# Half of a depthwise convolution moved from VectorE to GpSimd

## The chip, the cores and the metric

The kernel runs on one core of one Trainium2 chip. The metric is the device time of one execution in microseconds. Five engines work side by side on the core, each with its own instruction stream, and wait for each other through counted semaphores: TensorE (matmuls, PE in the profile; its weight loads are PEld), VectorE (DVE), ScalarE (ACT), GpSimd (POOL) and SyncE (SP), which here only issues the transfers of weights.

## The reference

The program is two transformer blocks in a row on 256 tokens of width 1024, all in float32. The second block has two layers and mixes tokens in four ways: Fourier, convolution, grouped attention, differential attention. The change touches only the convolution:

```python
def conformer_conv(z, w, bias, ln_g, ln_b):
    a, g = jnp.split(z, 2, axis=-1)
    u = a * jax.nn.sigmoid(g)                      # 256 tokens x 512 channels
    y = lax.conv_general_dilated(u, w[:, None, :], window_strides=(1,),
                                 padding=[(15, 15)],      # 31 taps
                                 feature_group_count=512) + bias
    return jax.nn.silu(layer_norm_2(y, ln_g, ln_b))

def mixer_stream(parts, ...):
    y_four = fourier_mix(zf) @ w_four              # branch 0
    y_conv = conformer_conv(...) @ w_conv          # branch 1
    ...                                            # branches 2 and 3: the attentions
    return sum(gates * [y_four, y_conv, y_gqa, y_diff]) @ w_out
```

Each channel has its own 31 weights (depthwise), and the layer norm runs over the 512 channels of a token.

## The kernel before

Activations lie transposed: channels on the 128 partitions, tokens along the free side, so 512 channels are four chunks of 128x256. Weights come in units of 128x2048 floats (1 MB), about 5.76 us of TensorE work each. Every product is made of three passes of a reduced float32 form: a value is split in a high part and a rest. For each weight unit ScalarE writes `w_high` (L343), VectorE writes `w_rest = raw - w_high` (L349), and TensorE multiplies high by high, high by rest and rest by high (L733). `w_high` has four buffers, `w_rest` two, so VectorE is at most one unit ahead.

The second block runs in passes: c0 (context, layer 0), x0 (tokens, layer 0), c1 (only keys and values) and x1 (tokens, layer 1). In c0, x0 and x1 ("full" passes) the order of the units is written by hand: conv_u, conv_g, four, q, kv, dq, dk, dv, gate0 (4 units), proj0 (2), gate1 (4), proj1 (2), then the attention "gqa", gate2, proj2, the attention "diff", gate3, proj3, out and the feed forward. `gateN` gives the gates of branch N, `projN` the projection of its result. Each engine has its own copy of this order, as calls of `linear(name, beside={unit: work})` (`cols_linear(..., before=...)` on TensorE): what stands in `beside` runs after the unit of that number.

The convolution: VectorE multiplies u by sigmoid (L2160), starts `acc` with the first tap and the bias for four chunks (L2163), and then does the other 30 taps as `acc += conv_in[shifted] * tap` with one scalar_tensor_tensor for each chunk and tap (L2087, in hardware loops, each waiting for the tap before it through `conv_step`). They are laid beside the units from four to proj0. When all are done (`taps_done`), TensorE sums `acc` over channels with a matrix of ones (L1167, `sum_acc`, ahead of gate1's unit 1), VectorE subtracts the mean (`conv_centre`, L2127 and L2128), ScalarE squares, TensorE sums again (`sum_squares`, ahead of unit 2), VectorE and ScalarE make the inverse root, VectorE scales (`conv_scale`), ScalarE applies silu, and `conv_split` (L2048) makes the operand of proj1. `merge_rows` multiplies the projection in the four PSUM banks with the gate (L1700) at the end of each branch; this frees the banks for the next unit.

In x0 and x1 gate1 also has the rotary embedding beside it (`swap_qk`, `rotate_q`, `rotate_d`). GpSimd builds tables in the first 225 us and later only writes rest parts of attention operands (L711). `rstd` is a 128x256 tile that norms use.

Of the kernel before, what the change touches and what calls it, by code (L numbers as in the profile page):

```python
# [136 lines left out]
def build(nc, t, out, consts):  # L137
    ctx = ExitStack()
    with ctx:
# [3 lines left out]
        def sem(name):  # L143
            return ctx.enter_context(nc.semaphore(name))
# [99 lines left out]
        def s5a(i):  # L244
# [62 lines left out]
        conv_a, conv_sig, conv_step, conv_st, conv_stc, conv_root, conv_n = [  # L307
            sem(x) for x in ("conv_a", "conv_sig", "conv_step", "conv_st", "conv_stc", "conv_root", "conv_n")]
# [187 lines left out]
        DVE_CHUNKS = HC  # L496
# [133 lines left out]
        def _(pool):  # L630
# [73 lines left out]

            for key in TASKS:
                for at in range(-1, len(TASKS[key])):
# [8 lines left out]
        def _(pe):  # L715
# [352 lines left out]
            for num, (p, l, s) in enumerate(PASSES):  # L1068
# [67 lines left out]
                def swap_dk():  # L1136
                    evacuated(pe, p + "dk")
                    pe.wait_ge(kd_dupc, num + 1)
                    pe.wait_ge(conv_n, 3 * nf + 2)
                    swap_halves(t1, HC, 2)  # L1140
# [29 lines left out]
                def sum_acc():  # L1170
                    pe.wait_ge(v_ready, num + 1)
                    conv_sums(1, acc, 0)

                def sum_squares():
                    conv_sums(2, oT, T)
# [6 lines left out]
                branch(0)  # L1182
                if rx is not None:
                    branch(1, gate_before={0: swap_qk, 1: sum_acc, 2: sum_squares, 3: lambda: (double_k(num), swap_dq())},
                           proj_before={1: swap_dk})
                    pe.wait_ge(d_rot, 3 * rx + 3)
                else:
                    branch(1, gate_before={1: sum_acc, 2: sum_squares, 3: lambda: double_k(num)})
# [28 lines left out]
        def _(act):  # L1217
# [262 lines left out]
            for num, (p, l, s) in enumerate(PASSES):  # L1480
# [73 lines left out]
                def conv_squares():  # L1554
                    act.wait_ge(conv_n, 3 * nf + 1)
                    A(oT, acc, ACT.Square).then_inc(conv_st, 1)
# [13 lines left out]
                branch(0)  # L1570
                branch(1, gate_beside={0: conv_squares, 1: conv_sqrt, 2: conv_silu, 3: lambda: doubled_out(num)})
# [33 lines left out]
        def _(dve):  # L1605
# [437 lines left out]
            for num, (p, l, s) in enumerate(PASSES):  # L2043
# [50 lines left out]
                def taps_done():  # L2094
# [70 lines left out]
                linear(p + "four", beside={0: lambda: taps(1, 2), 1: lambda: taps(3, 2)})  # L2165
                linear(p + "q", beside={0: lambda: taps(5, 2), 1: lambda: taps(7, 2)})
                linear(p + "kv", beside={0: lambda: taps(9, 2)})
                linear(p + "dq", beside={0: lambda: taps(11, 2), 1: lambda: (v_out(), taps(13, 2))})
                linear(p + "dk", beside={0: lambda: (fourier_split(), taps(15, 1)), 1: lambda: (mean_squares(), taps(16, 1))})
# [113 lines left out]
```

## Time and profile before

| | |
|---|---|
| median of 3 runs | 2777.2 us (2774.94 to 2777.76) |
| profiled execution | 2774.94 us, its span 2773.1 us |
| TensorE busy | 2354.6 us (85%) |
| VectorE busy | 1702.4 us (61%) |
| ScalarE busy | 1051.3 us (38%) |
| GpSimd busy | 278.4 us (10%) |
| taps on VectorE (L2087) | 360 instructions, 146.8 us busy, mean 477 ns |
| w_rest on VectorE (L349) | 311 instructions, 713.7 us busy, mean 2295 ns |
| chain that ended last | PE 67%, DVE 19%, ACT 4%, POOL 1% |

Busy is the time in which an engine executes; neighbouring instructions on one engine overlap a little in the records, so eight taps of 477 ns mean take 3.25 us. A wait is idle time of an engine, put down to the instruction that released it. The granted clock of TensorE is given as a share of 2.4 GHz: 1.0 or 0.5.

### The profile page before, as it was taken

To read this page: it belongs to the slowest core of one execution; us is meant where nothing else is said; L and a number is where in the kernel's file an instruction comes from. 1 tells how busy PE (TensorE), PEld (TensorE's weight loads), DVE (VectorE), ACT (ScalarE), POOL (GpSimd) and SP (SyncE) were. 2 spreads that over 40 slices of the span, in tenths; PEclk is the share of its full clock that TensorE was granted. 3 is DMA by queue.
4 is the path that set the end of the run, shared out by engine and by line. 5 is a ranking of instruction groups with operands and counts; after the bars stand their busy time and mean duration, and the time that the engine had idled before them with its cause. 6 is when DMAs were issued, how large, how long until landed. Compare 5 with 4: busy or idle time off the path is not lost.

```text
span 2773.1 us, 42565 instructions
## 1 busy us (share of the span) xinstructions
PE 2354.6 (85%) x17409; PEld 2181.0 (79%) x17409; DVE 1702.4 (61%) x2085; ACT 1051.3 (38%) x1202; POOL 278.4 (10%) x277
## 2 busy tenths in 40 slices
PE   4766688879999987769999988679999998776998
PEld 4621378879999987669999977479998997656998
DVE  5699734545548765555557965656545787555554
ACT  4200233444334444334344344334334435434432
POOL 3857200020000000100000001200000001110000
PEclk9878779979999998789999998779999999978999
DMA  5267624425555442135555432134545443113552
GB/s 164 94 268 307 240 94 139 150 65 169 182 191 157 143 148 69 56 120 168 181 175 153 152 106 67 40 98 153 182 161 158 152 146 98 61 45 108 171 178 91
DMA packets 282994, 388.31 MB, mean 140 GB/s; under 512 B 7847, under 2 KB 255966, under 8 KB 276703
## 3 DMA queue, kind: packets, MB, share of 16 engines
q1 hardware_dynamic: 279148, 379.40, 41.8%
q10 hardware_dynamic: 3282, 5.74, 0.6%
q8 instruction: 108, 1.77, 0.3%
q0 software_dynamic: 416, 1.08, 0.3%
q14 instruction: 40, 0.32, 0.0%
HBM read 385.04 MB, written 1.05 MB: 139 GB/s over the span
## 4 chain that ended last, share of the span: by engine, by line
PE 67%; DVE 19%; issue 4%; ACT 4%; POOL 1%; DVEq 0%; ACTq 0%
PE L L733 55%; PE M L733 5%; DVE w_rest L349 3%; DVE work L2087 2%; PE M L850 1%; POOL work_r L711 1%; DVE m L1891 1%; DVE gate L1891 1%; DVE work L2064 1%; DVE m L1706 1%; DVE gate L1700 1%; PE M L1092 1%; ACT w_high L343 1%; DVE work L2205 1%; PE L L877 1%
## 5 line engine op out<-in xcount | busy, mean ns | idle before, releaser
L733 PE MATMUL L<-n_high,w_high 128*128 128x256 f32 x3584 | 1055.0, 294 | 93.2 <-DVE n_rest L1644 42.2
L733 PE MATMUL L<-n_rest,w_high 128*128 128x256 f32 x3584 | 1039.9, 290 | 0.0
L733 PE MATMUL L<-n_high,w_rest 128*128 128x256 f32 x3584 | 1039.2, 290 | 0.0
L349 DVE TENSOR_TENSOR w_rest<-raw,w_high 128x2048 fp32r<-128x2048 f32 x311 | 713.7, 2295 | 382.9 <-PE L L733 347.9
L733 PEld LDWEIGHTS L<-n_high,w_high 128*128 128x128 f32 x3584 | 714.6, 199 | 115.6 <-issue 104.9
L343 ACT ACTIVATE w_high<-raw 128x2048 fp32r<-128x2048 f32 x311 | 594.0, 1911 | 502.7 <-PE L L733 432.2
L733 PEld LDWEIGHTS L<-n_rest,w_high 128*128 128x128 f32 x3584 | 715.3, 200 | 0.8
L733 PEld LDWEIGHTS L<-n_high,w_rest 128*128 128x128 f32 x3584 | 714.0, 199 | 0.0
L711 POOL TENSOR_TENSOR work_r<-kv,work_r 128x512 fp32r<-128x512 f32 (+2 forms) x44 | 63.6, 1449 | 2050.5 <-ACT work_r L1291 2050.5
L733 PE MATMUL M<-work_r 128*128 128x256 f32 (+3 forms) x744 | 170.8, 384 | 70.7 <-POOL work_r L711 35.6
L733 PEld LDWEIGHTS M<-work_r 64*128 64x128 f32 (+2 forms) x744 | 121.6, 215 | 106.8 <-issue 50.5
L733 PE MATMUL L<-hid_high,w_high 128*128 (+1 forms) x704 | 198.1, 281 | 6.1 <-DVE hid_rest L1988 6.1
L733 PE MATMUL L<-hid_rest,w_high 128*128 (+1 forms) x704 | 196.9, 280 | 0.0
L733 PE MATMUL L<-hid_high,w_rest 128*128 (+1 forms) x704 | 196.9, 280 | 0.0
L733 PE MATMUL L<-b_high,w_high 128*128 128x256 f32 x432 | 127.8, 296 | 50.0 <-ACT gate L1240 40.0
L2087 DVE SCALAR_TENSOR_TENSOR work<-work,tapc 128x256 f32<-128x256 f32 x360 | 146.8, 477 | 2.8 <-DVE work L2066 0.7
L733 PEld LDWEIGHTS L<-hid_high,w_high 128*128 128x128 f32 x704 | 134.3, 191 | 7.0 <-DVE hid_rest L1988 7.0
L1297 ACT ACTIVATE work<-M,soft 128x512 f32<-128x512 f32 (+1 forms) x104 | 62.6, 602 | 190.6 <-DVE soft L1716 190.5
L733 PEld LDWEIGHTS L<-hid_rest,w_high 128*128 128x128 f32 x704 | 134.0, 190 | 0.1
L733 PEld LDWEIGHTS L<-hid_high,w_rest 128*128 128x128 f32 x704 | 133.8, 190 | 0.0
L1716 DVE TENSOR_REDUCE soft<-M 128x1 f32<-128x512 f32 (+1 forms) x104 | 60.5, 586 | 118.7 <-PE M L733 118.7
L733 PEld LDWEIGHTS L<-b_high,w_high 128*128 128x128 f32 x432 | 87.3, 202 | 52.6 <-issue 41.7
(339 smaller groups left out, 2850.4 us busy)
## 6 DMA issues: line engine op xcount, KB each, us to landing
raw<-in_w_in SPq DMA_DIRECT2D x116, 1024.0 KB, 5.4
raw<-in_w_ffn SPq DMA_DIRECT2D x99, 1024.0 KB, 5.2
raw<-in_w_ada SPq DMA_DIRECT2D x48, 1024.0 KB, 8.1
raw<-in_w_out SPq DMA_DIRECT2D x16, 1024.0 KB, 5.0
raw<-in_w_gate SPq DMA_DIRECT2D x11, 1024.0 KB, 5.3
raw<-in_w_up SPq DMA_DIRECT2D x11, 1024.0 KB, 5.3
raw<-in_w_down SPq DMA_DIRECT2D x11, 1024.0 KB, 5.0
raw<-in_w_four SPq DMA_DIRECT2D x6, 1024.0 KB, 5.0
```

Source lines behind the costliest of these rows:

```text
L343: nc.scalar.activation(w_high[:, u.first % 4, :], raw[:, u.first % 4, :], ACT.Copy).then_inc(high_ready, 1)
L349: nc.vector.tensor_tensor(w_rest[:, u.first % 2, :], raw[:, u.first % 4, :], w_high[:, u.first % 4, :].bitcast(F32), ALU.subtract).then_in ...
L711: nc.gpsimd.tensor_tensor(rest, src, high.bitcast(F32), ALU.subtract).then_inc(op_rest, 1)
L733: ins = mm(dst, a, b, start=first and i == 0, stop=last and i == 2, skip_group_check=skip)
L850: ins = mm(M[:, 0, 0:T], ones[:, :], m[:, c, :], start=c == 0, stop=c == DC - 1)
L877: ins = nc.tensor.transpose(turned_bank[x["group"] % 2][:, c * P:(c + 1) * P], exps[(i - x["map"]) % 3][:, c * P:(c + 1) * P], ident[:, :])
L1092: ins = mm(M[:, c // 2, c % 2 * T:(c % 2 + 1) * T], y1[:, c, a, k * P:(k + 1) * P], dft256[:, k, a, :], start=i == 0, stop=i == 3)
L1297: A(exps[i % 3][:, 0:nk], score_bank[x["g"] % 2][:, 0:nk], ACT.Exp, bias=soft[:, x["g"] % 4, 0:1], accum_out=soft[:, x["g"] % 4, 2:3]).the ...
L1700: V.tensor_tensor(pair(m if first else gate, b), pair(gate, b), L[:, b, :], ALU.mult).then_inc(bank_free[b], 1)
L1716: V.tensor_reduce(soft[:, x["g"] % 4, 0:1], score_bank[x["g"] % 2][:, 0:nk], AX.X, ALU.max, negate=True).then_inc(neg_max, 1)
L1891: V.tensor_tensor_scan(dst[:, r, :], s5c[:, 0, tile + r:tile + r + 1].to_broadcast((P, T)), src[:, r, :], 0.0, ALU.mult, ALU.add).then_inc ...
L2087: V.scalar_tensor_tensor(acc[:, c, :], conv_in[:, c, bass.ds(k, T)], tapc[:, l, bass.ds(4 * k + c, 1)], acc[:, c, :], ALU.mult, ALU.add).t ...
```

## The change

Of the four chunks VectorE keeps the taps of two. GpSimd gets those of the other two: it has no scalar_tensor_tensor here, so each tap is a multiplication into `rstd` and an addition into `acc`, every one waiting for the one before (`conv_pool`). VectorE still starts all four chunks. The order around it moves too: VectorE's taps end in gate0; both channel sums move from gate1 to proj0, the first ahead of its first unit, and with it the wait for GpSimd; centre, square and root move into proj0, the scaling to gate1's first unit. The squares go to `t2` instead of `oT`.

```diff
-        DVE_CHUNKS = HC
+        DVE_CHUNKS = 2
         CONV_STEPS = HC + DVE_CHUNKS * (TAPS - 1)
@@ GpSimd
+            def taps(nf, l):
+                mine, tmp = HC - DVE_CHUNKS, rstd[:, :]
+                base = nf * (TAPS - 1) * mine * 2 + 1
+                pool.wait_ge(conv_step, CONV_STEPS * nf + HC)
+                if nf == 0:
+                    pool.sem_inc(conv_pool, 1)
+                with pool.Fori(1, TAPS) as k:
+                    for i in range(mine):
+                        c, at = DVE_CHUNKS + i, base + (k - 1) * mine * 2 + 2 * i
+                        pool.wait_ge(conv_pool, at)
+                        nc.gpsimd.tensor_tensor(tmp, conv_in[:, c, bass.ds(k, T)],
+                                                tapc[:, l, bass.ds(4 * k + c, 1)].to_broadcast((P, T)), ALU.mult).then_inc(conv_pool, 1)
+                        pool.wait_ge(conv_pool, at + 1)
+                        nc.gpsimd.tensor_tensor(acc[:, c, :], acc[:, c, :], tmp, ALU.add).then_inc(conv_pool, 1)
             for key in TASKS:
+                if kind_of(key) == "gqa":
+                    taps(FULL_OF[key[:2]], 0 if key[1] == "0" else 1)
@@ TensorE
                 def swap_dk():
-                    pe.wait_ge(conv_n, 3 * nf + 2)
                 def sum_acc():
+                    pe.wait_ge(conv_pool, (nf + 1) * (TAPS - 1) * (HC - DVE_CHUNKS) * 2 + 1)
                     pe.wait_ge(v_ready, num + 1)
                     conv_sums(1, acc, 0)
-                branch(0)
+                branch(0, proj_before={0: sum_acc, 1: lambda: conv_sums(2, t2, T)})
-                    branch(1, gate_before={0: swap_qk, 1: sum_acc, 2: sum_squares, 3: ...}, proj_before={1: swap_dk})
+                    branch(1, gate_before={0: swap_qk, 3: ...}, proj_before={1: swap_dk})
@@ ScalarE
-                    A(oT, acc, ACT.Square).then_inc(conv_st, 1)
+                    A(t2[:, 0:HC, :], acc, ACT.Square).then_inc(conv_st, 1)
-                branch(0)
-                branch(1, gate_beside={0: conv_squares, 1: conv_sqrt, 2: conv_silu, 3: lambda: doubled_out(num)})
+                branch(0, proj_beside={0: conv_squares, 1: conv_sqrt})
+                branch(1, gate_beside={0: conv_silu, 3: lambda: doubled_out(num)})
@@ VectorE
-                linear(p + "four", beside={0: lambda: taps(1, 2), 1: lambda: taps(3, 2)})
...
+                linear(p + "four", beside={0: lambda: taps(1, 3), 1: lambda: taps(4, 3)})
+                linear(p + "q", beside={0: lambda: taps(7, 3), 1: lambda: taps(10, 3)})
+                linear(p + "kv", beside={0: lambda: taps(13, 4)})
+                linear(p + "dq", beside={0: lambda: taps(17, 4), 1: lambda: (v_out(), taps(21, 4))})
+                linear(p + "dk", beside={0: lambda: (fourier_split(), taps(25, 3)), 1: mean_squares})
+                linear(p + "dv", beside={0: lambda: normed(HC), 1: lambda: normed(0)})
-                gl(0, {0: lambda: (normed(1), taps(19, 1)), 1: lambda: (normed(2), taps(20, 1)),
-                       2: lambda: (last_norm(), taps(21, 1)), 3: lambda: taps(22, 2)},
-                   {0: lambda: taps(24, 3), 1: lambda: (taps(27, 4), taps_done())})
+                gl(0, {0: lambda: normed(1), 1: lambda: normed(2), 2: last_norm, 3: last_taps},
+                   {0: conv_centre, 1: conv_mean_square})
-                    gl(1, {0: conv_centre, 1: conv_mean_square, 2: conv_scale, 3: conv_split})
+                    gl(1, {0: conv_scale, 2: conv_split})
-                    gl(1, {0: conv_centre, 1: lambda: (rotate_q(), conv_mean_square()), 2: lambda: (rotated_q(), conv_scale()),
-                           3: lambda: (rotate_d(0, dq, dq), conv_split())},
+                    gl(1, {0: conv_scale, 1: rotate_q, 2: lambda: (rotated_q(), conv_split()), 3: lambda: rotate_d(0, dq, dq)},
```

GpSimd between the attention of the first block and the first attention of pass c0, before (a hardware loop is printed once; every row writes the rest of an attention operand):

```order
L711 TENSOR_TENSOR work_r<-kv,work_r 128x512
L711 TENSOR_TENSOR work_r<-work,work_r 128x512
L711 TENSOR_TENSOR work_r<-kv,work_r 128x512 x4
L711 TENSOR_TENSOR work_r<-kv,work_r 128x256
L711 TENSOR_TENSOR work_r<-work,work_r 128x256 x2
```

and now:

```order
L730 TENSOR_TENSOR work_r<-kv,work_r 128x512 x4
L712 UNCONDITIONAL_BRANCH
L712 ISA
L716 ISA
L716 REGISTER_ALU
L716 TENSOR_TENSOR rstd<-work,tapc 128x256
L718 REGISTER_ALU
L719 TENSOR_TENSOR work<-work,rstd 128x256
L715 REGISTER_ALU
L716 ISA
L716 TENSOR_TENSOR rstd<-work,tapc 128x256
L718 REGISTER_ALU
```

The loop runs 30 times with two multiplications (L716) and two additions (L719) each; `work` holds conv_in and acc. It is queued ahead of the attention operands of its pass.

VectorE from proj0's first unit to the product at its end in c0, before (`taps`, 16 instructions, stand right ahead of the product):

```order
L2087 SCALAR_TENSOR_TENSOR work<-work,tapc 128x256
L2083 REGISTER_ALU
L2083 COMPARE_AND_BRANCH
L1700 TENSOR_TENSOR m<-gate,L 128x512 x4
L349 TENSOR_TENSOR w_rest<-raw,w_high 128x2048
L2127 TENSOR_SCALAR rstd<-M 128x256
L2128 TENSOR_TENSOR work<-work,rstd 128x1024
L349 TENSOR_TENSOR w_rest<-raw,w_high 128x2048
L2133 TENSOR_SCALAR rstd<-M 128x256
```

and now:

```order
L2098 COMPARE_AND_BRANCH
L349 TENSOR_TENSOR w_rest<-raw,w_high 128x2048
L2143 TENSOR_SCALAR rstd<-M 128x256
L2144 TENSOR_TENSOR work<-work,rstd 128x1024
L349 TENSOR_TENSOR w_rest<-raw,w_high 128x2048
L2149 TENSOR_SCALAR rstd<-M 128x256
L1715 TENSOR_TENSOR m<-gate,L 128x512 x4
```

The taps end a unit earlier, and centre and mean square stand ahead of the product (L1715, L1700 before) instead of behind it.

TensorE where gate0 ends and proj0 begins in c0, before (`n_high` is gate0's operand, `b_high` proj0's):

```order
L733 MATMUL L<-n_high,w_high 128x256
L733 MATMUL L<-n_rest,w_high 128x256
L733 MATMUL L<-n_high,w_rest 128x256
L733 MATMUL L<-b_high,w_high 128x256
L733 MATMUL L<-b_rest,w_high 128x256
```

and now:

```order
L752 MATMUL L<-n_high,w_high 128x256
L752 MATMUL L<-n_rest,w_high 128x256
L752 MATMUL L<-n_high,w_rest 128x256
L1185 MATMUL M<-work,ones 128x256 x4
L752 MATMUL L<-b_high,w_high 128x256
L752 MATMUL L<-b_rest,w_high 128x256
```

The channel sum stands ahead of proj0, and all of TensorE's later work behind the sum's wait.

## Rows read from the trace of the kernel before

**Rows 1.** The page: busy us (share of the span), instructions

```profile
PE 2354.6 (85%) x17409; PEld 2181.0 (79%) x17409; DVE 1702.4 (61%) x2085; ACT 1051.3 (38%) x1202; POOL 278.4 (10%) x277
```

**Rows 2.** Window, length; busy PE, PEld, DVE, ACT, POOL; PEclk, DMA, GB/s (c0, x1)

```profile
878.90:975.55 96.65, 95.87 (x754) 94.12 (x752) 82.27 (x118) 42.58 (x41) 0.00 (x0) 1.00 0.49 153
...
2154.35:2250.98 96.63, 95.86 (x752) 94.10 (x752) 82.23 (x118) 42.59 (x41) 0.00 (x0) 1.00 0.49 153
```

**Rows 3.** Timeline of VectorE, end of proj0 in c0: start us, length us, what

```profile
986.80 6.42 DVE L2087 SCALAR_TENSOR_TENSOR work<-work,tapc 128x256 f32<-128x256 f32 x16
993.36 2.48 DVE L1700 TENSOR_TENSOR m<-gate,L 128x512 f32<-128x512 f32 x4
```

**Rows 4.** Waits of TensorE, c0, 976 to 1050: us, times, longest

```profile
PE L L733 <- DVE m L1700: 7.1, 1, 7.1
...
PE L L733 <- ACT gate L1240: 2.0, 1, 2.0
```

**Rows 5.** Waits of TensorE, x0, 1540 to 1640

```profile
PE L L733 <- DVE m L1700: 5.0, 1, 5.0
...
PE L L733 <- DVE b_rest L2048: 1.1, 1, 1.1
PE L L733 <- ACT gate L1240: 0.8, 1, 0.8
```

**Rows 6.** Busy time by engine right after the wait of rows 4

```profile
992.30:999.10 6.80, 4.91 (x23) 4.94 (x24) 5.68 (x8) 1.91 (x1) 0.00 (x0) 0.50 0.01 2
```

**Rows 7.** Timeline of GpSimd, 78 to 85

```profile
79.69 2.67 POOL L666 TENSOR_TENSOR kv<-s5w 128x256 f32<-128x256 f32 x1
...
83.85 0.74 POOL L669 TENSOR_TENSOR kv<-s5w 128x256 f32<-128x256 f32 x1
```

**Rows 8.** Timeline of GpSimd, 116 to 142

```profile
117.82 0.68 POOL L697 TENSOR_TENSOR dup<-s5w,kv 128x256 f32<-128x256 f32 x1
118.58 0.78 POOL L699 TENSOR_TENSOR s5w<-s5w,dup 128x256 f32<-128x256 f32 x1
...
134.70 2.55 POOL L697 TENSOR_TENSOR dup<-s5w,kv 128x256 f32<-128x256 f32 x1
...
138.14 0.62 POOL L697 TENSOR_TENSOR dup<-s5w,kv 128x256 f32<-128x256 f32 x1
```

**Rows 9.** Sequencer instructions of the tap loop on VectorE: ns min/median/max

```profile
L2087 DVEq FUSED_REGOPS  x276: 93/93/118, 878.0 to 2267.1; - x138
L2087 DVEq ALU_OP  x23: 40/40/40, 2153.6 to 2266.2; - x23
```

**Rows 10.** Timeline of VectorE, 116 to 142

```profile
117.95 0.84 DVE L1644 SCALAR_TENSOR_TENSOR n_rest<-m,flat,n_high 128x256 fp32r<-128x256 f32 x1
...
119.58 0.84 DVE L1644 SCALAR_TENSOR_TENSOR n_rest<-m,flat,n_high 128x256 fp32r<-128x256 f32 x1
...
133.95 2.81 DVE L349 TENSOR_TENSOR w_rest<-raw,w_high 128x2048 fp32r<-128x2048 f32 x1
```

**Rows 11.** Groups of VectorE, 878.9 to 975.55: busy us, mean ns, idle before

```profile
L2087 DVE SCALAR_TENSOR_TENSOR work<-work,tapc 128x256 f32<-128x256 f32 x87 | 35.7, 478 | 0.9 <-DVE work L2059 0.2 <-DVE work L2066 0.2
L349 DVE TENSOR_TENSOR w_rest<-raw,w_high 128x2048 fp32r<-128x2048 f32 x15 | 34.3, 2287 | 12.3 <-PE L L733 12.3
```

**Rows 12.** Timeline of VectorE, start of the taps in c0

```profile
877.53 1.38 DVE L2163 TENSOR_SCALAR work<-work,tapc,cols 128x256 f32<-128x256 f32 x4
...
881.03 3.25 DVE L2087 SCALAR_TENSOR_TENSOR work<-work,tapc 128x256 f32<-128x256 f32 x8
```

**Rows 13.** Timeline of ScalarE: evictions of two neighbouring units

```profile
875.58 0.60 ACT L1240 ACTIVATE work<-L 128x512 f32<-128x512 f32 x1 [3.36 <-PE L L733]
...
881.34 0.60 ACT L1240 ACTIVATE work<-L 128x512 f32<-128x512 f32 x1 [3.35 <-PE L L733]
```

**Rows 14.** Timeline of GpSimd, 171 to 184, beside VectorE's scans

```profile
173.09 0.98 POOL L699 TENSOR_TENSOR s5w<-s5w,dup 128x256 f32<-128x256 f32 x1
174.15 0.88 POOL L697 TENSOR_TENSOR dup<-s5w,kv 128x256 f32<-128x256 f32 x1
```

More of the change, by code:

```diff
@@ L306, in build @@
         z_ready, four1, four1c, four2 = sem("z_ready"), sem("four1"), sem("four1c"), sem("four2")
-        conv_a, conv_sig, conv_step, conv_st, conv_stc, conv_root, conv_n = [
-            sem(x) for x in ("conv_a", "conv_sig", "conv_step", "conv_st", "conv_stc", "conv_root", "conv_n")]
+        conv_a, conv_sig, conv_step, conv_st, conv_stc, conv_root, conv_n, conv_pool = [
+            sem(x) for x in ("conv_a", "conv_sig", "conv_step", "conv_st", "conv_stc", "conv_root", "conv_n", "conv_pool")]
         qk_sq, qk_sum, qk_ms, qk_root, qk_n, qk_rot, d_rot, kd_dup, kd_dupc = [
@@ L1170, in sum_acc @@
                 def sum_acc():
+                    pe.wait_ge(conv_pool, (nf + 1) * (TAPS - 1) * (HC - DVE_CHUNKS) * 2 + 1)
                     pe.wait_ge(v_ready, num + 1)
                     conv_sums(1, acc, 0)
-                def sum_squares():
-                    conv_sums(2, oT, T)
                 def branch(i, gate_before={}, proj_before={}, start=0):
@@ L1180, in branch @@
                     acc_linear(p + f"proj{i}", b_high, b_rest, before=proj_before)
-                branch(0)
+                branch(0, proj_before={0: sum_acc, 1: lambda: conv_sums(2, t2, T)})
                 if rx is not None:
-                    branch(1, gate_before={0: swap_qk, 1: sum_acc, 2: sum_squares, 3: lambda: (double_k(num), swap_dq())},
-                           proj_before={1: swap_dk})
+                    branch(1, gate_before={0: swap_qk, 3: lambda: (double_k(num), swap_dq())}, proj_before={1: swap_dk})
                     pe.wait_ge(d_rot, 3 * rx + 3)
                 else:
-                    branch(1, gate_before={1: sum_acc, 2: sum_squares, 3: lambda: double_k(num)})
+                    branch(1, gate_before={3: lambda: double_k(num)})
                 pe.wait_ge(kd_dupc, num + 1)
@@ L2092, in last_norm, with last_taps @@
                     dve.sem_inc(qk_n, 1)
-                def taps_done():
+                def last_taps():
+                    taps(28, 3)
                     dve.wait_ge(conv_step, CONV_STEPS * (nf + 1))
@@ L2164, in _ @@
                                     ALU.mult, ALU.add).then_inc(conv_step, 1)
-                linear(p + "four", beside={0: lambda: taps(1, 2), 1: lambda: taps(3, 2)})
[L2166 to L2169, printed above, removed]
-                linear(p + "dv", beside={0: lambda: (normed(HC), taps(17, 1)), 1: lambda: (normed(0), taps(18, 1))})
+                linear(p + "four", beside={0: lambda: taps(1, 3), 1: lambda: taps(4, 3)})
[4 more added lines that the diff above has]
+                linear(p + "dv", beside={0: lambda: normed(HC), 1: lambda: normed(0)})
                 evacuated(dve, p + "dv")
```

## The prediction

> **What bounds the kernel now.** I read the page's busy shares first [rows 1]: TensorE is busy 85% of the span, VectorE 61%, GpSimd 10%. An average says little about a change in one place, so the next view is the busy time of the stretch that the change touches. It lies between the end of the first conv tap (chunk starts, L2163) and the first matmul of proj0, three times in the program (passes c0, x0, x1), and is 96.65 us long each time [rows 2]. TensorE is busy 95.87 us of it; the weights it needs (w_rest from VectorE, L349) are never late; GpSimd does nothing. So before proj0 VectorE is not the bound, and taking taps from it there gives nothing. It becomes the bound once, right behind proj0: VectorE runs 16 taps from 986.80, and only then, at 993.36, the product gate*L (L1700) that frees TensorE's banks [rows 3]. TensorE waits 7.1 us for it in c0 [rows 4] and 5.0 us in x0 [rows 5] (x1 has the same row). At the end of gate1 stand two small waits: 2.0 us for ScalarE in c0, 1.1 us for b_rest in x0 and x1 [rows 4, 5].
>
> **What the change can gain.** With the taps of two chunks gone from VectorE, 60 of 120 scalar_tensor_tensor per pass are left there (the last six in gate0), proj0 holds only centre and mean square, and the product L1700 starts when proj0 ends. c0: 7.1 falls to about the 0.7 that the product's first quarter and a wake-up take (2.48 us for four [rows 3]), a gain of 6.4; in x0 and x1 five rope matmuls stand there and cover it, a gain of 5.0 each. The end of gate1 falls to the 0.8 us that an ordinary eviction costs TensorE [rows 5]: 1.2 in c0, 0.3 in x0 and in x1. Sum: 7.6 + 5.3 + 5.3 = 18.2 us. After the wait TensorE ran at half clock for 6.8 us, 4.91 of them busy [rows 6], which cost some 2.4; the change takes this dip away, but, as below, makes a longer wait with a dip of its own, so I count both as nothing. The eight sum matmuls per pass are moved, not added.
>
> **What it adds: the chain on GpSimd.** Per pass 30 taps x 2 chunks x 2 instructions (multiply into rstd, add into acc) = 120, each waiting for the one before it. TensorE's first sum, now ahead of proj0, waits for the last one, and proj0, and with it the whole of the weights' pipeline, is queued behind that wait.
> A multiply of 128x256 with a broadcast input takes 0.62 us with VectorE silent [rows 8], an add of two plain 128x256 tiles 0.74 [rows 7], and 0.08 lies between two linked instructions (117.82 + 0.68 to 118.58 [rows 8]). A pair is 0.62 + 0.74 + 0.16 = 1.52 us, 60 pairs 91.2 us. That alone would just fit in 96.65.
> The loop computes the number it waits for, and the multiply has a register instruction that waits. VectorE's own tap loop shows 93 ns and 40 ns for such two [rows 9]. GpSimd's are in no trace; between nothing (hidden under the add) and twice that I take 0.133 us x 60 = 8.0 us, the nearest row.
> VectorE's scalar_tensor_tensor with both inputs in SBUF: beside these the multiply takes 0.68, not 0.62 [rows 8]. 60 taps and five from the q and k norms: 65 x 0.06 = 3.9 us.
> VectorE's w_rest (128x2048, both inputs in SBUF) stops GpSimd altogether: the same subtraction took 2.67 us with one beside it and 0.74 without [rows 7], and L697 took 2.55 at 134.70 where w_rest stood beside it from 133.95 [rows 8, 10]. Each costs 1.93 us. Fifteen lie in the stretch [rows 11] and one more, for proj0's second unit, is issued ahead of the sums: 16 x 1.93 = 30.9 us.
> GpSimd's chain is thus 91.2 + 8.0 + 3.9 + 30.9 = 134.0 us from the same starting point, against 96.65 that TensorE needs to get there: 37.4 us late, and 0.1 for the wake-up, 37.5 per pass, 112.5 in three. While TensorE stands, no weight unit is finished and VectorE makes no more w_rest, so the tail of the chain runs undisturbed, which the count of 16 has in it.
>
> **The Trainium skill on this.** The trace shows a w_rest stopping GpSimd for 1.93 us, but a scalar_tensor_tensor costing it only 0.06. "SBUF — State Buffer", § Summary: rules for kernel authors, says that a VectorE instruction with two SBUF inputs and a GpSimd instruction that reads SBUF exclude each other, the second to issue blocking until the first is done; on w_rest the trace agrees, on the short instructions the row decides, since most of their time falls in GpSimd's own gaps. By that rule in full the short ones would cost their whole length, which is a rival below.
>
> **The other way round.** VectorE is held up too: eight taps took 3.25 us alone [rows 12], but beside GpSimd two scalar_tensor_tensor took 119.58 - 117.95 = 1.63 us [rows 10], 0.81 each instead of 0.41, and a w_rest 2.81 instead of 2.29 [rows 10, 11]. A unit with six taps then takes VectorE 2.3 + 0.5 + 4.9 = 7.7 us, where TensorE takes 5.76 (two evictions, 875.58 and 881.34 [rows 13]). Up to dk the 54 taps cost 43.7 instead of the 24.6 of 60 today, ten w_rest 5 more: 24 in all, of which VectorE's 12.3 idle us [rows 11] take half. TensorE comes to proj0 some 12 us late. This adds nothing, since GpSimd is 37 late there; it only shortens the visible wait to about 25 us.
>
> **Sum.** 112.5 - 18.2 = +94.3 us. The profiled execution took 2774.94 (span 2773.1), so 2869; the median of the runs is 2777.2, 0.1% from it, and I leave 2869.
>
> **Bounds.** Below: no loop cost gives 24 less, 2845; if half of each w_rest's block were hidden, 46 less on top, 2799. Above: beside VectorE's scans the two forms took 0.88 and 0.98 [rows 14]; a pair at that rate is 0.88 + 0.98 + 0.16 + 0.13 = 2.15, 129.0 + 30.9 = 159.9 per pass, 78 more than the forecast, 2947. I stay with the undisturbed and the scalar_tensor_tensor rows because those are the instructions that stand beside it here.
>
> **Rivals.**
> Forecast, GpSimd is late at proj0 in every pass: 80%. For it: every price but the loop's has a row, and even without loop and short instructions the chain is 122 us against 96.65.
> The short instructions block in full: 65 x 0.41 = 26.7 instead of 3.9 per pass, 68 more, 2937; or the scan rate, 2947. For it: the scans did slow both forms by a third. Against it: beside scalar_tensor_tensor the two forms stood at 0.68 and 0.78 [rows 8]. 10%.
> The stall is smaller, because the blocks overlap with gaps or loop costs: 2800 to 2830. 3%.
> Faster: GpSimd's chain is done before TensorE comes. It decides at one point, a pair with all that is added to it at or under 96.65 / 60 = 1.61 us; now I count 2.23. If w_rest stopped nothing and the loop cost nothing, the chain would be 91.2 + 3.9 = 95.1, and the waits behind proj0 would go: up to 18.2 less, 2757. Against it stand two separate rows with a stopped instruction. 4%.
> No change: the chain fits, but VectorE's 12 us of lateness per pass take the 18.2 back: about 2777. 3%.
>
> **Numbers.** Likeliest 2869. What a measurement of this kernel can tell from no change is 0.2%, 5.6 us. Slower has the forecast, the blocking in full and the smaller stall, 93%; faster 4%, same 3%. The range goes from 2830 (no loop cost and a sixth of w_rest's block hidden) to 2937 (the blocking in full).
>
> **What the profile after would show.** GpSimd busy about 300 to 370 us more in all; its multiplies at 0.62 to 0.70 and adds at 0.74 to 0.80, each some 2 us longer where a w_rest stands beside it; per pass some 134 us from first multiply to last add. TensorE waits for GpSimd's add ahead of the sum matmuls, 20 to 40 us in each of three passes. The waits for L1700's product behind proj0 are under 1 us. VectorE's taps last 0.8 us apiece while GpSimd runs, and TensorE waits a few us in all for w_rest in the units from four to dk. I am wrong if the last add ends before gate0's last matmul (then the block or the prices don't hold), or if pairs take over 2.1 us apart from w_rest (then the blocking in full does).

## The result and the profile after

The changed kernel takes 2865.15 us (median of 4 runs, 2861.9 to 2871.57), the kernel before 2777.48 beside it, which is 87.7 us more. Over all 21 runs of the changed kernel (median 2868.19, 2860.69 to 2872.38) the ratio is 1.0325 with a 95% interval of 1.0311 to 1.0339: 3.25% slower. The profiled executions stand further apart, 2871.57 against 2774.94 us, that is +96.6; the forecast was +94.3, to 2869.

The busy shares of the page, after (engine, busy us, share, instructions), and the engines' shares of the chain that ended last:

```profile
PE 2368.6 (83%) x17409; PEld 2185.6 (76%) x17409; DVE 1712.3 (60%) x1905; ACT 1051.3 (37%) x1202; POOL 621.4 (22%) x637
...
PE 61%; DVE 14%; POOL 13%; issue 3%; ACT 3%; POOLq 1%; DVEq 0%; ACTq 0%
```

GpSimd is busy 343 us more than in [rows 1], of which 342.9 are the two forms below, and it has 13% of the chain that ended last, where it had 1%. VectorE has 180 instructions fewer and is busy 10 us longer: beside GpSimd the same instruction takes it longer (a tap 824 ns in the mean, where it was 477). The groups of the page (count, busy us, mean ns, idle before):

```profile
L716 POOL TENSOR_TENSOR rstd<-work,tapc 128x256 f32 x180 | 178.0, 989 | 980.3 <-DVE work L2179 670.3
...
L719 POOL TENSOR_TENSOR work<-work,rstd 128x256 f32<-128x256 f32 x180 | 164.9, 916 | 14.1
...
L2102 DVE SCALAR_TENSOR_TENSOR work<-work,tapc 128x256 f32<-128x256 f32 x180 | 136.6, 824 | 0.0
```

The waits of TensorE in c0, 860 to 1090 us, where [rows 4] were before (us in total, times, longest):

```profile
PE M L1185 <- POOL work L719: 29.6, 1, 29.6
...
PE M L1127 <- DVE b_rest L2063: 2.7, 1, 2.7
PE L L752 <- DVE w_rest L349: 2.4, 2, 1.2
PE L L752 <- DVE m L1715: 0.9, 1, 0.9
PE L L752 <- ACT gate L1255: 0.8, 1, 0.8
```

The wait of 7.1 us for the product behind proj0 is 0.9 now, the 2.0 at the end of gate1 are 0.8, and one wait of 29.6 for GpSimd's last add stands ahead of proj0. In x0 and x1 it is 30.5 and 31.2, 91.3 in all. Three windows of c0: up to the last matmul of gate0, the wait, and what follows (length; busy PE, PEld, DVE, ACT, POOL; PEclk, DMA, GB/s), beside [rows 2, 6]:

```profile
879.40:984.13 104.73, 99.55 (x752) 96.49 (x750) 97.32 (x89) 41.82 (x39) 90.16 (x87) 0.97 0.48 146
984.13:1013.70 29.57, 0.01 (x1) 0.03 (x1) 3.58 (x3) 2.40 (x2) 24.17 (x34) 0.58 0.16 52
1013.70:1020.50 6.80, 6.79 (x27) 6.05 (x27) 1.65 (x2) 1.06 (x1) 0.00 (x0) 0.56 0.00 0
```

VectorE is busy 97.32 of 104.73 us, where it was busy 82.27 of 96.65 with all the taps. TensorE ends gate0 8.9 us later than before (104.76 us after the chunk starts, not 95.86): 5.1 us of it are the waits for b_rest and w_rest above, and in the rest it runs below the full clock (0.97 in the mean, 1.00 before). Then TensorE does nothing for 29.57 us, VectorE works 3.58 of them, and GpSimd finishes alone. After the wait TensorE's granted clock is near the lower of its two levels (0.56) for 6.8 us.

The start of GpSimd's chain (start us, length us, what, idle before it) and its end:

```profile
879.97 2.08 POOL L716 TENSOR_TENSOR rstd<-work,tapc 128x256 f32 x1 [266.17 <-POOLq L711]
882.13 0.80 POOL L719 TENSOR_TENSOR work<-work,rstd 128x256 f32<-128x256 f32 x1
883.14 0.61 POOL L716 TENSOR_TENSOR rstd<-work,tapc 128x256 f32 x1 [0.21 <-POOL work L719]
883.83 0.80 POOL L719 TENSOR_TENSOR work<-work,rstd 128x256 f32<-128x256 f32 x1
884.92 0.86 POOL L716 TENSOR_TENSOR rstd<-work,tapc 128x256 f32 x1 [0.29 <-POOL work L719]
885.86 0.81 POOL L719 TENSOR_TENSOR work<-work,rstd 128x256 f32<-128x256 f32 x1
886.88 2.41 POOL L716 TENSOR_TENSOR rstd<-work,tapc 128x256 f32 x1 [0.21 <-POOL work L719]
...
1012.88 0.72 POOL L719 TENSOR_TENSOR work<-work,rstd 128x256 f32<-128x256 f32 x1
```

and VectorE's timeline there, to be laid beside it, with its last instructions before and first after the wait:

```profile
885.98 2.83 DVE L349 TENSOR_TENSOR w_rest<-raw,w_high 128x2048 fp32r<-128x2048 f32 x1
888.74 4.57 DVE L2102 SCALAR_TENSOR_TENSOR work<-work,tapc 128x256 f32<-128x256 f32 x6
...
985.79 2.34 DVE L349 TENSOR_TENSOR w_rest<-raw,w_high 128x2048 fp32r<-128x2048 f32 x1 [0.42 <-DVE work L2102]
1017.49 0.42 DVE L2143 TENSOR_SCALAR rstd<-M 128x256 f32<-128x256 f32 x1 [29.36 <-PE M L1185]
```

The multiply of 886.88 was issued while the w_rest of 885.98 to 888.81 ran, and ended at 889.29, 0.48 behind it: most of its 0.61 us of work came when w_rest had gone. The other rows are a pair with its gaps: 0.61 to 0.86 for a multiply, 0.80 for an add, 0.08 between them, and 0.21 or 0.29 ahead of a multiply, where a register instruction of the loop waits for the add first.

**Where the time stands.** I measured each pass from the end of the chunk starts (L2163, L2179) to the first matmul of proj0, and to the first transpose of the attention behind gate1 and proj1:

| us | proj0, c0 / x0 / x1 | attention, c0 / x0 / x1 | sum of the three | rest of the span |
|---|---|---|---|---|
| before | 96.6 / 96.6 / 96.6 | 166.6 / 168.0 / 168.7 | 503.3 | 2269.8 |
| after | 137.5 / 137.1 / 137.6 | 196.0 / 200.2 / 201.3 | 597.5 | 2272.1 |

The three stretches are 94.2 us longer, and the rest of the program 2.3: nothing of note happened elsewhere.

### The profile page after: what moved, and what is told of

It reads as the page before. It is cut to its first block, busy times and chain, and to the rows that moved or that the text cites. A ratio compares the mean times of both kernels' runs of the same rounds, so it can differ in the third digit from the quotient of the medians.

```text
span 2869.6 us, 43346 instructions
## 1 busy us (share of the span) xinstructions
PE 2368.6 (83%) x17409; PEld 2185.6 (76%) x17409; DVE 1712.3 (60%) x1905; ACT 1051.3 (37%) x1202; POOL 621.4 (22%) x637
## 4 chain that ended last, share of the span: by engine, by line
PE 61%; DVE 14%; POOL 13%; issue 3%; ACT 3%; POOLq 1%; DVEq 0%; ACTq 0%
PE L L752 51%; POOL rstd L716 6%; POOL work L719 6%; PE M L752 5%; DVE w_rest L349 1%; PE M L869 1%; POOL work_r L730 1%; DVE m L1906 1%; DVE gate L1906 1%; DVE m L1721 1%; DVE gate L1715 1%; DVE work L2219 1%; DVE s5z L1901 1%; PE L L896 1%; ACT w_high L343 1%
## 5 line engine op out<-in xcount | busy, mean ns | idle before, releaser
L349 DVE TENSOR_TENSOR w_rest<-raw,w_high 128x2048 fp32r<-128x2048 f32 x311 | 728.0, 2341 | 388.1 <-PE L L752 339.5
L716 POOL TENSOR_TENSOR rstd<-work,tapc 128x256 f32 x180 | 178.0, 989 | 980.3 <-DVE work L2179 670.3
L730 POOL TENSOR_TENSOR work_r<-kv,work_r 128x512 fp32r<-128x512 f32 (+2 forms) x44 | 63.7, 1451 | 810.9 <-ACT work_r L1306 810.9
L719 POOL TENSOR_TENSOR work<-work,rstd 128x256 f32<-128x256 f32 x180 | 164.9, 916 | 14.1
L752 PE MATMUL L<-b_high,w_high 128*128 128x256 f32 x432 | 130.3, 302 | 45.3 <-ACT gate L1255 37.6
L2102 DVE SCALAR_TENSOR_TENSOR work<-work,tapc 128x256 f32<-128x256 f32 x180 | 136.6, 824 | 0.0
```

Of the source, the lines that this page charges most:

```text
L349: nc.vector.tensor_tensor(w_rest[:, u.first % 2, :], raw[:, u.first % 4, :], w_high[:, u.first % 4, :].bitcast(F32), ALU.subtract).then_in ...
L716: nc.gpsimd.tensor_tensor(tmp, conv_in[:, c, bass.ds(k, T)], tapc[:, l, bass.ds(4 * k + c, 1)].to_broadcast((P, T)), ALU.mult).then_inc(co ...
L719: nc.gpsimd.tensor_tensor(acc[:, c, :], acc[:, c, :], tmp, ALU.add).then_inc(conv_pool, 1)
L730: nc.gpsimd.tensor_tensor(rest, src, high.bitcast(F32), ALU.subtract).then_inc(op_rest, 1)
L752: ins = mm(dst, a, b, start=first and i == 0, stop=last and i == 2, skip_group_check=skip)
L2102: V.scalar_tensor_tensor(acc[:, c, :], conv_in[:, c, bass.ds(k, T)], tapc[:, l, bass.ds(4 * k + c, 1)], acc[:, c, :], ALU.mult, ALU.add).t ...
```

## Experiments

Eight kernels ran. Each is named by what it changes against the kernel after, or against the one before where it says so. "Pass" means c0, x0 and x1 as above, and a stage sum is the sum of the table's fourth column.

**1. The new order without GpSimd.** Is anything of the loss in the moved sums, norm and scaling? GpSimd's loop and TensorE's wait for it are left out, and nobody does these taps: VectorE keeps its half.

```diff
-                if kind_of(key) == "gqa":
-                    taps(FULL_OF[key[:2]], 0 if key[1] == "0" else 1)
@@ TensorE, sum_acc
-                    pe.wait_ge(conv_pool, (nf + 1) * (TAPS - 1) * (HC - DVE_CHUNKS) * 2 + 1)
```

> The changed kernel without GpSimd's tap loop and without TensorE's wait for it: the 30 later taps of chunks 2 and 3 are left out, the new order of sums, centre and scaling stays. Theory (GpSimd's chain is the whole loss): the waits behind proj0 are gone (18.2 us) and so are the clock dips (up to 7 us), 2750 to 2760. Rival (the moved sums and their wait cost by themselves): 2777 or more.

2748.38 us, 0.9907 (0.9890 to 0.9923) of the kernel before. TensorE reaches proj0 at +97.2 us, and its waits in c0 behind that are:

```profile
PE L L750 <- DVE m L1712: 0.9, 1, 0.9
PE L L750 <- ACT gate L1252: 0.8, 1, 0.8
```

The moved order, with half the taps on VectorE, costs nothing. It gives 26 us (0.93%), more than the 18.2 of the prediction's first part; the half-clock stretch behind the old wait, which that part left out, is some 2.4 more per pass by the prediction's own estimate from [rows 6]. All of the loss of after comes with GpSimd's chain, and the chain swallows this gain as well.

**2. The chain without VectorE's taps.** Is the time set by GpSimd alone? VectorE's 60 taps per pass are left out.

```diff
-        CONV_STEPS = HC + DVE_CHUNKS * (TAPS - 1)
+        CONV_STEPS = HC
@@ VectorE
                 def taps(k0, n_):
-                    with dve.Fori(k0, k0 + n_) as k:
-                        ...
+                    return None
```

> The changed kernel without VectorE's 60 taps per pass (left out), GpSimd's loop kept. Theory (VectorE's and TensorE's lateness of 9 us per pass lies inside GpSimd's chain and adds nothing; only the 4 to 5 us per pass by which VectorE's taps slow GpSimd go): chain 129 instead of 133.6 us, TensorE's visible wait for it grows from 30 to about 35 us, time 2850 to 2855. Rival (the lateness adds in full): about 2825.

2861.86 us, 1.0305 (1.0284 to 1.0327): the number that was expected, 2850 to 2855, was missed. The profiled spans differ by 9.6 us (2860.0 and 2869.6), and the stages by 13.6 in sum. The chain is 129.9 us in c0, 3.7 shorter than after. TensorE is no longer held up (it ends gate0 at +95.85), so more of the same chain shows as its wait:

```profile
PE M L1185 <- issue: 34.7, 1, 34.7
```

The releaser is not named in this record, but the wait stands at the same line and ends behind the last add. Without 60 of VectorE's taps the time hardly moves, so the rival in which VectorE's load sets it (2825) falls, and a tap of VectorE costs GpSimd's chain some 0.06 us in the mean (3.7 / 60), not its whole length.

**3. No input for w_rest.** Is it the subtraction's two inputs in SBUF that stop GpSimd? In the units from four to proj0 a memset fills w_rest instead.

```diff
+            if u.first in CHEAP:
+                nc.vector.memset(w_rest[:, u.first % 2, :].bitcast(F32), 0.0).then_inc(rest_ready, 1)
+                return
             nc.vector.tensor_tensor(w_rest[:, u.first % 2, :], raw[:, u.first % 4, :], ...
```

> The changed kernel where VectorE fills w_rest of the units from four to proj0 in the full passes with a constant (memset, no SBUF input) instead of subtracting; the rest part of these weights is left out. Theory (each of 16 subtractions per pass stops GpSimd for 1.85 us): no GpSimd instruction over 1.4 us in the loop, chain 104 us, visible wait under 10 us per pass, time 2775 to 2785. Rival (GpSimd is that slow by itself, or any VectorE instruction stops it): chain 125 or more, time 2845 or more.

2818.63 us, 1.0153 (1.0136 to 1.0169): missed by 34 us. The chain is 116.1 us and the wait in c0 20.2. The cause is in the timelines. GpSimd:

```profile
890.75 2.46 POOL L725 TENSOR_TENSOR work<-work,rstd 128x256 f32<-128x256 f32 x1
...
897.16 2.07 POOL L722 TENSOR_TENSOR rstd<-work,tapc 128x256 f32 x1 [0.21 <-POOL work L725]
```

and VectorE:

```profile
890.58 1.76 DVE L353 MEMSET w_rest<- 128x2048 f32 x1 [0.38 <-DVE work L2108]
...
896.72 1.76 DVE L353 MEMSET w_rest<- 128x2048 f32 x1 [0.38 <-DVE work L2108]
```

The memset, which reads nothing, stopped GpSimd as well, in 7 of its 16 per pass, each time up to the memset's end. What sets these seven apart is open: in c0 five of them come 0.38 us behind a tap of VectorE, but so do two that stopped nothing. So this kernel did not take away what it was meant to, and did not answer its question. It needed another instruction in that place.

**4. That instruction: a reduction.** A tensor_reduce reads the raw weights, 128x2048, and writes one column; w_rest keeps an old value. The cut shows it against the kernel of experiment 3.

```diff
-                nc.vector.memset(w_rest[:, u.first % 2, :].bitcast(F32), 0.0).then_inc(rest_ready, 1)
+                nc.vector.tensor_reduce(stats[:, 0, 0:1], raw[:, u.first % 4, :], AX.X, ALU.max).then_inc(rest_ready, 1)
```

> As e3, but in place of the subtraction VectorE takes a maximum over the same raw tile (tensor_reduce, one SBUF input of 128x2048, a 128x1 output) for the units from four to proj0 of the full passes; w_rest keeps old values there, so the rest part of these weights is left out. In e3 the filling still stopped GpSimd 7 times in 16. Theory (what stops GpSimd is the two-input form, and each of 16 costs 1.85 us): no GpSimd instruction over 1.4 us in the loop, chain 103 to 106 us, visible wait 5 to 10 us per pass, the three stages 29 us shorter each than in the changed kernel, time 2775 to 2785. Rival (any long VectorE instruction stops GpSimd): chain 130 or more, 2855 or more.

2782.14 us, 1.0015 (1.0005 to 1.0026): as expected. The reduction keeps VectorE for 2.27 us, as long as the subtraction (2.29), in the same place, but GpSimd runs through it:

```profile
885.37 2.27 DVE L353 TENSOR_REDUCE stats<-raw 128x1 f32<-128x2048 f32 x1
```

```profile
885.37 0.61 POOL L722 TENSOR_TENSOR rstd<-work,tapc 128x256 f32 x1 [0.21 <-POOL work L725]
886.07 0.73 POOL L725 TENSOR_TENSOR work<-work,rstd 128x256 f32<-128x256 f32 x1
887.08 0.61 POOL L722 TENSOR_TENSOR rstd<-work,tapc 128x256 f32 x1 [0.29 <-POOL work L725]
```

In the whole trace no multiply takes over 0.962 us and no add over 0.986; the chain is 105.1 us, 28.5 less than after. The groups of GpSimd in c0, after:

```profile
L716 POOL TENSOR_TENSOR rstd<-work,tapc 128x256 f32 x60 | 58.8, 980 | 280.8 <-POOLq L711 266.2 <-POOL work L719 14.6
L719 POOL TENSOR_TENSOR work<-work,rstd 128x256 f32<-128x256 f32 x60 | 55.5, 926 | 4.7
```

and in this kernel:

```profile
L725 POOL TENSOR_TENSOR work<-work,rstd 128x256 f32<-128x256 f32 x60 | 46.1, 769 | 4.7
L722 POOL TENSOR_TENSOR rstd<-work,tapc 128x256 f32 x60 | 39.7, 662 | 280.7 <-POOLq L717 266.1 <-POOL work L725 14.6
```

The gaps are the same to a tenth of a microsecond, 14.6 and 4.7; the 28.5 us are all in the instructions. This shows the step of the prediction that carries most: the subtraction stops GpSimd, a same long reduction does not.

The reduction differs from the subtraction in two things: it has one input, and it writes almost nothing. Which of them counts can be read from other instructions of VectorE in this trace. `b_rest` is also a subtraction that writes a full tile, but one of its inputs lies in PSUM:

```profile
932.51 1.21 DVE L2069 TENSOR_TENSOR b_rest<-M,b_high 128x1024 fp32r<-128x1024 f32 x1
```

```profile
932.72 0.74 POOL L725 TENSOR_TENSOR work<-work,rstd 128x256 f32<-128x256 f32 x1
```

The add was issued and ended inside it at its usual length, in c0 as in x0 and x1 (0.741 to 0.745 us). The reciprocals (128x256, one input, 1.74 us) held no instruction inside them over 0.742 us either. A full-width write alone does not stop GpSimd here; what the subtraction has beyond `b_rest` is the second input in SBUF, and twice the columns. The columns do not matter: a tap, 128x256 with two inputs in SBUF, holds GpSimd up in the same way, as shown below.

Even so the chain is longer than the 96.65 us that TensorE needs, and TensorE still waits 8.5 us in c0:

```profile
PE M L1191 <- POOL work L725: 8.5, 1, 8.5
```

**5. The wait later.** The sums, and with them the wait for GpSimd, go back to gate1, as before; the rest is as after.

```diff
-                branch(0, proj_before={0: sum_acc, 1: lambda: conv_sums(2, t2, T)})
+                branch(0)
-                    branch(1, gate_before={0: swap_qk, 3: ...}, proj_before={1: swap_dk})
+                    branch(1, gate_before={0: swap_qk, 1: sum_acc, 2: lambda: conv_sums(2, oT, T), 3: ...}, ...)
@@ VectorE
-                gl(0, {0: lambda: normed(1), 1: lambda: normed(2), 2: last_norm, 3: last_taps},
-                   {0: conv_centre, 1: conv_mean_square})
+                gl(0, {0: lambda: normed(1), 1: lambda: normed(2), 2: last_norm, 3: last_taps})
-                    gl(1, {0: conv_scale, 2: conv_split})
+                    gl(1, {0: conv_centre, 1: conv_mean_square, 2: conv_scale, 3: conv_split})
...
```

> The changed kernel with both channel sums, centre, squares, root, scaling and the wait for GpSimd where they were before (gate1), taps split as in the change. Theory (the loss is deadline minus chain): TensorE comes to the wait 18 us later (proj0 and gate1's first unit), two or three more subtractions lengthen the chain by 4 to 5 us, so each wait falls from 30 to about 15 us, time 2815 to 2830. Rival (the place of the wait does not matter, the load does): 2860.

2828.26 us, 1.0190 (1.0173 to 1.0207): as expected. TensorE's waits in c0:

```profile
PE M L1186 <- POOL work L719: 16.1, 1, 16.1
...
PE L L752 <- ACT gate L1256: 2.8, 2, 2.0
```

Proj0 and gate1's first unit now lie beside the chain. They are some 17 us of TensorE's work, and the wait falls by only 13.5, since two more w_rest come into the chain (18 stopped instructions, 137.9 us). What covers the wait also lengthens it. In the stages this gives 45.2 us back (597.5 to 552.3).

**6. One chunk instead of two.**

```diff
-        DVE_CHUNKS = 2
+        DVE_CHUNKS = 3
```

> The changed kernel with three chunks of taps on VectorE and one on GpSimd. GpSimd's chain has 60 instructions: about 51 us, some 8 blocks of 1.85 and a few for the taps, 70 us, well inside 96.65, so TensorE should not wait for it. Theory (the two engines hold each other up): VectorE's taps take 0.76 us apiece while GpSimd runs, so a unit with nine of them takes 9.6 us against TensorE's 5.76, w_rest comes late, 15 to 25 us per pass, time 2815 to 2845. Rival (only the length of GpSimd's chain counts): it fits, and the gains of 18.2 come through, 2757.

2807.44 us, 1.0110 (1.0090 to 1.0130): faster than after, 8 us below the range that was expected, and still slower than before. GpSimd's chain is 73.3 us and done long before proj0; TensorE's waits in c0:

```profile
PE L L752 <- DVE w_rest L349: 8.9, 3, 4.8
PE M L1127 <- DVE b_rest L2063: 4.5, 1, 4.5
```

and VectorE at the start:

```profile
883.18 6.18 DVE L2102 SCALAR_TENSOR_TENSOR work<-work,tapc 128x256 f32<-128x256 f32 x9
889.28 2.70 DVE L349 TENSOR_TENSOR w_rest<-raw,w_high 128x2048 fp32r<-128x2048 f32 x1
891.90 6.14 DVE L2102 SCALAR_TENSOR_TENSOR work<-work,tapc 128x256 f32<-128x256 f32 x9
```

Nine taps and a subtraction take 8.7 us, where TensorE takes 5.76 a unit: a tap costs 0.68 us beside GpSimd, not the 0.41 of [rows 12]. TensorE reaches proj0 at +117.8, 21 us late, with nobody waiting for GpSimd: 13.4 are the waits above, and most of the rest is TensorE below the full clock (0.94 in the mean from the chunk starts to the end of gate0, 1.00 before). A rival in which only the length of GpSimd's chain counts asked for 2757; it falls. The loss has two sides, and the smaller share of taps uncovers the second. The order beside the units was made for two chunks and puts nine taps beside one unit here, so this run does not show what one chunk would give in an order of its own.

**7. Taps earlier, all on VectorE.** The gain in the first part of the prediction needs no GpSimd: VectorE had 12.3 us of idle time ahead of proj0 [rows 11]. Against the kernel before, four more taps (16 instructions) stand beside dq's first unit, and none is left beside proj0's second.

```diff
-                linear(p + "dq", beside={0: lambda: taps(11, 2), 1: lambda: (v_out(), taps(13, 2))})
+                linear(p + "dq", beside={0: lambda: taps(11, 6), 1: lambda: (v_out(), taps(17, 2))})
...
-                   {0: lambda: taps(24, 3), 1: lambda: (taps(27, 4), taps_done())})
+                   {0: lambda: (taps(28, 3), taps_done())})
```

> The kernel before, all taps on VectorE, but four more taps (16 instructions, 6.4 us) beside dq's first unit, where VectorE idled 7.2 us, and so none beside proj0's second. Theory (the wait behind proj0 is the 16 last taps and nothing else): 7.1, 5.0 and 5.0 us fall to 0.7 and 0, and the half clock behind them goes, 2753 to 2762. Rival (VectorE, busy 82 of 96.65 us, then delays a weight unit between dq and proj0 by as much): 2775 or more.

2753.4 us, 0.9919 (0.9900 to 0.9938), the fastest kernel with the whole computation. VectorE in the two places:

```profile
909.49 9.58 DVE L2087 SCALAR_TENSOR_TENSOR work<-work,tapc 128x256 f32<-128x256 f32 x24
919.94 2.29 DVE L349 TENSOR_TENSOR w_rest<-raw,w_high 128x2048 fp32r<-128x2048 f32 x1 [0.87 <-PE L L733]
...
986.39 2.48 DVE L1700 TENSOR_TENSOR m<-gate,L 128x512 f32<-128x512 f32 x4
```

The product starts at 986.39, not 993.36 [rows 3], and of TensorE's waits there this is left:

```profile
PE L L733 <- ACT gate L1240: 2.8, 2, 2.0
PE L L733 <- DVE m L1700: 0.9, 1, 0.9
```

Twenty-four tap instructions (six taps) beside one unit still leave VectorE idle for 0.87 us before the next subtraction, and TensorE reaches proj0 at +96.6 as before.

**8. The sums earlier too.** On top of 7, two more taps earlier and sums and norm one step earlier, so that the last wait for ScalarE at the end of gate1 goes.

```diff
-                   {0: lambda: (taps(28, 3), taps_done())})
+                   {0: conv_centre})
...
-                branch(0)
+                branch(0, proj_before={1: sum_acc})
```

> As e6 with all taps on VectorE, two more taps moved into its idle time (beside q's second and dk's second unit), so that the last tap stands beside gate0's last unit, the first channel sum ahead of proj0's second unit, the second ahead of gate1's first, the rest of the norm one unit earlier. Theory (only the waits at the end of gate1 and a dip behind them are left to gain, 1.2 to 4 us in c0, 0.3 to 1.2 in x0 and x1): 2745 to 2752. Rival (VectorE is now full, 95.4 of 96.65 us, and w_rest comes late at proj0): above e6, 2760.

2757.57 us, 0.9936 (0.9923 to 0.9950): missed, and no better than 7 (the intervals overlap). By stages c0 is 3.4 us shorter, x0 2.5 and x1 4.2 longer. In x0 and x1 one wait is new:

```profile
PE M L1124 <- DVE work L2114: 2.0, 1, 2.0
```

The rotary embedding stands there beside the norm in x0 and x1, and not in c0. It is most of the 2.5. In x1 TensorE also runs slower from proj0 to the attention (0.95 of the full clock in the mean, 0.98 in experiment 7), which over 68 us is some 2 us more; why it does so there is open.

## Why the prediction was right

**The chain on GpSimd, 134.0 us forecast.** The trace has 133.6, 133.3 and 133.9 us in the three passes. Its parts in c0:

| | forecast | measured |
|---|---|---|
| quiet instructions | 60 x (0.62 + 0.74) = 81.6 | 60 x (0.613 + 0.722) = 80.1 |
| gaps, links and loop | 9.6 + 8.0 = 17.6 | 4.7 + 14.6 = 19.3 |
| stopped by w_rest | 16 x 1.93 = 30.9 | 16 instructions, 29.5 (1.85 each) |
| beside short instructions | 3.9 | 4.7 |
| sum | 134.0 | 133.6 |

Each part is within 2 us, and the misses cancel; that the sum is within 0.4 us is luck. The loop, the only price without a row, cost more than was taken: 0.25 us ahead of a multiply in the mean, where 0.08 and 0.13 for the loop were forecast, while the gap before an add was 0.08 as in [rows 8]. GpSimd's sequencer in that loop, after (ns, min/median/max):

```profile
L716 POOLq FUSED_REGOPS  x180: 74/77/89, 879.7 to 2350.1; - x180
...
L716 POOLq ALU_OP  x90: 35/35/45, 879.8 to 2348.5; - x90
```

These two are a little shorter than VectorE's in [rows 9], but the time from an add's end to the next multiply's start, with all that lies in it, is 0.21 or 0.29.

**What stops GpSimd, and what a tap costs it.** This carried the forecast against its main rival. After shows 16 stopped instructions per pass (11 multiplies, 5 adds, 2.08 to 2.75 us each in c0), as many as w_rest was expected to stand beside, and experiment 4, without the subtraction, none. The short scalar_tensor_tensor cost it little: taking 60 of them away (experiment 2) shortened the chain by 3.7 us, where the rival had 26.7 for 65. That rival, 2937, falls, and so does the one at the rate beside the scans: outside the stops a multiply took up to 0.87 and an add 0.81.

But the reason is not that a tap blocks less than a subtraction. Two of VectorE's taps, to be laid beside GpSimd's multiply of 884.92 and add of 885.86 above:

```profile
884.84 0.47 DVE L2102 SCALAR_TENSOR_TENSOR work<-work,tapc 128x256 f32<-128x256 f32 x1
```

```profile
885.23 0.83 DVE L2102 SCALAR_TENSOR_TENSOR work<-work,tapc 128x256 f32<-128x256 f32 x1
```

The multiply was issued while the first tap ran and took 0.86 instead of 0.61, ending 0.47 behind the tap, as it ends 0.48 behind a subtraction. The second tap was issued while the multiply ran and took 0.83 instead of 0.47, ending 0.28 behind it. The whole trace of after has this, counted where one was issued at least 0.02 us behind the start of the other and 0.14 before its end:

| issued | while this ran | times | ended behind it by, us |
|---|---|---|---|
| multiply on GpSimd | a subtraction | 31 | 0.468 to 0.476 |
| multiply on GpSimd | a tap | 27 | 0.468 to 0.477 |
| add on GpSimd | a subtraction | 13 | 0.580 to 0.604 |
| add on GpSimd | a tap | 85 | 0.581 to 0.611 |
| tap on VectorE | an instruction of GpSimd's loop | 117 | 0.277 to 0.285 |
| subtraction on VectorE | an instruction of GpSimd's loop | 33 | 2.144 to 2.153 |

However much of the first was left, the second ended at nearly the same distance behind it. So the later of the two waits for the earlier, and nearly in full, short or long. The subtraction of 885.98, issued while an add had 0.68 us to go, took 2.83 us; one issued while GpSimd paused (942.46) took 2.28. A tap costs GpSimd little because it is itself the one that waits most of the time: it then runs mostly in the pause between two of GpSimd's instructions, and little of it is left when the next one is issued. The Trainium skill, "SBUF — State Buffer", § Summary: rules for kernel authors, says that the second of two such instructions to issue waits for the whole of the first, and this trace agrees for both. The prediction read that rule as the whole length of every tap on GpSimd's side. That step was wrong, though its price, taken from the row, was right: the rule in full fits what was measured.

**The place of the wait.** GpSimd's last add in c0 ends at 1013.60, 134.2 us after the chunk starts. TensorE needed 96.65, so it is 37.6 late against the kernel before (forecast 37.5). Behind it stands the first channel sum, eight matmuls at half clock in 3.18 us (1013.71 to 1016.89; 3.19 in x0 and x1), moved here from gate1; with it the table's 137.5 comes out.

**The gain.** From proj0 to the attention c0, x0 and x1 went from 70.0, 71.4 and 72.1 us to 58.5, 63.1 and 63.7, 28.2 less. TensorE's idle time in these stretches fell from 38.2 to 20.1 us, which is 18.1, forecast 18.2. Another 4.6 are the first sum, which took 1.54 us in each at full clock (1002.19 to 1003.73 in c0) and is now ahead of proj0. The 5.5 that are left are matmuls at a higher clock: the granted clock over these stretches was 0.91 to 0.93 before and is 0.96 to 0.97 now, with the old half-clock stretch behind the wait gone. The way to proj0 is 40.9 + 40.5 + 41.0 = 122.4 us longer in the three; 3 x 3.19 = 9.6 of this is the sum, 5.0 more than it cost before since it stands in the new stretch near half clock, and without it the way is 112.8 longer, forecast 112.5. The difference of 122.4 and 28.2 is the 94.2 us of the table.

**Where only the size was off.** VectorE's lateness was priced at 12 us per pass and was 8.9 in c0 (gate0 ends at 104.76 and not 95.86), 7.6 and 7.4 in x0 and x1, so the visible wait was 30 us and not 25. A tap beside GpSimd took 0.76 us (six in 4.57), not 0.81. It changed nothing in the sum, because GpSimd was later still, as the prediction said. Experiment 6 shows what this term is worth where it is uncovered: 21 us per pass.

**The clock.** Both dips were counted as nothing. After the wait of after TensorE ran at 0.56 for 6.8 us, after the wait of before at 0.50 for as long [rows 6]. By the split above the old one gave back up to 5.5 us in the three passes and the new one took 5.0 at the sum, so they nearly cancel. No run separates them, and the forecast had no ground for it beyond the likeness of the two, so here too some luck is in the 94.2.

**Profile and median.** The profiled execution of after was the slowest of its four runs (2871.57). The forecast of 2869, which was made against profiled executions, was within 3 us of it, 4 us above the median of these four (2865.15) and 1 us above that of all 21 (2868.19).

**Faster, or no change.** Both rivals needed a pair of 1.61 us. A pair took 2.23 in c0 (133.6 / 60), and 1.75 (105.1 / 60) even where no subtraction stopped GpSimd (experiment 4). This shows two grounds. Two chunks are too many for GpSimd in 96.65 us even where no subtraction stops it, which by itself takes the gain away (1.0015 of before); and the subtraction stops it 16 times, which makes the loss. That a tap takes two instructions on GpSimd is how this kernel is written; no run shows whether it could be one.

## What to carry to other kernels

Work given to GpSimd is priced by what VectorE does at that time, and by who issues first. Add up the long VectorE instructions with two SBUF inputs in the stretch: each costs GpSimd its remaining length. A row of short ones costs GpSimd little (0.06 us a tap here) and VectorE much: up to twice their length. Put the result against the time that the consumer leaves, not against busy shares: VectorE was 61% busy and not the bound where the taps stood. And before work is moved to another engine, look whether the one late instruction can be mended by order: four taps (16 instructions) moved to where VectorE was idle gave 0.8%, and the move to GpSimd cost 3.2%.

## What the hardware showed that was not expected

- A memset on VectorE (128x2048, 1.765 us, no input) stopped GpSimd in 7 of 16 cases per pass, up to 2.46 us for an add of 0.72; a tensor_reduce over 128x2048 with one input (2.27 us) did so in none of 16 per pass. Which memsets stop it is open.
- Of a VectorE instruction with two inputs in SBUF and an instruction of GpSimd's loop the later waits for the earlier, on either engine, short or long: a GpSimd multiply ended 0.47 to 0.48 us behind the VectorE instruction that was under way, tap or subtraction, and a tap 0.28 behind the GpSimd instruction. VectorE's tap went from 0.41 us [rows 12] to 0.76 (two chunks on GpSimd) or 0.68 (one chunk), the subtraction from 2.29 to 2.8 where it was issued into a GpSimd instruction.
- In the hardware loop on GpSimd 0.21 to 0.29 us stand between an add and the next multiply, ahead of which a register instruction (74 to 89 ns) waits for the add; 0.08 stands where there is no such instruction.
